# Splitting weight units in halves of two k-tiles, and one sigmoid issued four units later, in a two-block fp32 transformer kernel

## What is computed

```python
def first_block(x, p, ...):
    a = rms_norm(h, norm_mix_pre)
    z = a @ w_in                                   # 2048 x 4656
    y_lru = rglru_mixer(u, g_lru, ...)
    y_nsa = nsa_mixer(q, kc, vc, ksel, vsel, kw, vw, gts, ...)
    h = h + rms_norm(y @ w_out, norm_mix_post)
    f = square(relu(rms_norm(h) @ mlp_w1)) @ mlp_w2    # 2048 x 8192 and back
    h = h + rms_norm(f, norm_mlp_post)
    h = h + sigmoid(h @ ple_gate) * (p @ ple_proj)
def second_block(x, c, ctx, ...):                  # two layers, each on x and on the context ctx
    shift, scale, gate = split(silu(c) @ w_mod + b_mod, 3)
    q, k, v, g_att, u_pool, g_pool, a_conv, b_conv, g_conv = split(hx @ w_in_2, ...)   # 2048 x 6656
    u = a_conv * sigmoid(b_conv); y = depthwise_conv31(u); ...
    y = concat(y_att * silu(g_att), y_pool * silu(g_pool), y_conv * silu(g_conv)) @ w_out_2
```

## Time and profile before

| | |
|---|---|
| median of 3 runs | 2902.8 us |
| the profiled execution's own time | 2906.9 us |
| its span, first to last instruction | 2905.1 us |
| TensorE busy | 2795.1 us, 96% |
| VectorE, ScalarE, GpSimd busy | 1680.8, 1237.5, 316.7 us |
| chain that ended last | TensorE 61%, VectorE 7%, ScalarE 2%, DMA 1% |

### The profile page before, as it was taken

One profiled execution on the slowest core, in us unless ns is written; L12 is line 12 of the kernel. 1 busy time (PEld: TensorE's weight loads), 2 busy tenths in 40 slices (PEclk: granted clock), 3 DMA queues, 4 the chain that ended last, 5 costly groups with the idle time before them and its releaser, 6 DMA issues.

```text
span 2905.1 us, 32293 instructions
## 1 busy us (share of the span) xinstructions
PE 2795.1 (96%) x13403; PEld 2188.4 (75%) x13403; DVE 1680.8 (58%) x1906; ACT 1237.5 (43%) x1493; POOL 316.7 (11%) x260
## 2 busy tenths in 40 slices
PE   4999899999979999999999999999999999999998
PEld 3777788888857777777777787887778788777776
DVE  3545455655545556555444564558885654678754
ACT  3444224544443333333343443444555444444543
POOL 1000100000013000000000020024200011312001
PEclk9999799999989999999999999999999999999999
DMA  6877466446577776676777666565444655553453
GB/s 217 282 252 265 153 210 207 152 145 244 189 245 255 277 243 233 234 248 219 270 250 240 231 212 218 202 231 166 153 134 170 206 185 196 169 168 131 163 172 129
DMA packets 292353, 600.29 MB, mean 207 GB/s; under 512 B 12482, under 2 KB 19210, under 8 KB 290032
## 3 DMA queue, kind: packets, MB, share of 16 engines
q1 hardware_dynamic: 278272, 545.69, 55.6%
q0 software_dynamic: 10960, 49.10, 4.7%
q10 hardware_dynamic: 2976, 3.45, 0.4%
HBM read 585.02 MB, written 13.17 MB: 206 GB/s over the span
## 4 chain that ended last, share of the span: by engine, by line
PE 61%; DVE 7%; ACT 2%; DMA 1%; issue 1%; POOL 0%; ACTq 0%; POOLq 0%; DVEq 0%
PE ps L639 17%; PE ps L641 17%; PE ps L640 17%; DVE wlo L1793 3%; PE ps L650 2%; DVE bvx L2314 2%; ACT whi L1229 1%; PE ps L1043 1%; PE ps L1061 1%; DVE ex L2294 0%; PE ps L1130 0%; PE ps L1154 0%; PE ps L621 0%; PE ps L863 0%; DMA h_d<-h 0%
## 5 line engine op out<-in xcount | busy, mean ns | idle before, releaser
L1793 DVE TENSOR_TENSOR wlo<-raw,whi 128x2048 fp32r<-128x2048 f32 x420 | 973.9, 2319 | 996.2 <-ACT whi L1229 995.4
L1229 ACT ACTIVATE whi<-raw 128x2048 fp32r<-128x2048 f32 x420 | 797.4, 1899 | 1376.6 <-PE ps L641 1165.6
L639 PE MATMUL ps<-whi,ay_hi 128*128 128x512 f32 x1728 | 689.9, 399 | 12.3 <-DVE wlo L1793 8.1
L639 PE MATMUL ps<-whi,ax_hi 128*128 128x512 f32 (+1 forms) x1632 | 652.6, 400 | 25.0 <-DVE wlo L1793 22.7
L641 PE MATMUL ps<-whi,ay_lo 128*128 128x512 f32 x1728 | 675.0, 391 | 0.0
L640 PE MATMUL ps<-wlo,ay_hi 128*128 128x512 f32 x1728 | 674.4, 390 | 0.0
L641 PE MATMUL ps<-whi,ax_lo 128*128 128x512 f32 (+1 forms) x1632 | 637.0, 390 | 0.0
L640 PE MATMUL ps<-wlo,ax_hi 128*128 128x512 f32 (+1 forms) x1632 | 636.1, 390 | 0.0
L639 PEld LDWEIGHTS ps<-whi,ax_hi 128*128 128x128 f32 x1632 | 310.8, 190 | 134.1 <-issue 59.2
L639 PEld LDWEIGHTS ps<-whi,ay_hi 128*128 128x128 f32 x1728 | 325.4, 188 | 94.3 <-issue 14.5
L641 PEld LDWEIGHTS ps<-whi,ay_lo 128*128 128x128 f32 x1728 | 325.1, 188 | 69.4
(11 more groups left out here) (475 smaller groups left out, 1998.1 us busy)
## 6 DMA issues: line engine op xcount, KB each, us to landing
raw<-in_w_in_dram SPq DMA_DIRECT2D x208, 1024.0 KB, 5.1
raw<-in_mlp_w_dram SPq DMA_DIRECT2D x128, 1024.0 KB, 6.4
raw<-in_w_mod_dram SPq DMA_DIRECT2D x96, 1024.0 KB, 7.4
raw<-in_w_out_dram SPq DMA_DIRECT2D x64, 1024.0 KB, 5.1
raw<-in_ple_gate_dram SPq DMA_DIRECT2D x16, 1024.0 KB, 5.1
z2c<-zsc POOLq DMA_DIRECT2D x13, 512.0 KB, 3.3
h<-in_x_dram POOLq DMA_DIRECT2D x2, 2048.0 KB, 10.7
G<-bias_d ACTq DMA_DIRECT2D x4, 768.0 KB, 6.3
```

What stands on the lines that cost most here:

```text
L639: mm(dst, hi_[:, kk, tt], whi[:, x.s % 2, k, 0:w], start=(nth == 0), stop=False)
L1229: A(whi[:, x.s % 2, :, 0:w], raw[:, x.slot, :, 0:w], ACT.Copy).then_inc(hi_ready, 1)
L1793: V.tensor_tensor(wlo[:, x.s % 2, :, 0:w], raw[:, x.slot, :, 0:w], f32v(whi[:, x.s % 2, :, 0:w]), ALU.subtract).then_inc(lo_ready, 1)
```

## The change

Splitting, handing over and freeing go by halves of two k-tiles. ScalarE makes `whi` in two instructions of 1024 elements, each after the same half of unit s-2 has been used; VectorE makes `wlo` in two; TensorE waits for each half apart. `lo_ready`, `hi_ready` and `unit_used` count halves, so every wait on them elsewhere is doubled. TensorE's order inside a unit stays "rows first" in the first and the last unit of a chunk (`by_rows`), and is "half first" in the two between: there the first half of the weights is free in the middle of the unit, and in `by_rows` units after three quarters. ScalarE's sigmoid of `cb` moves from position 0 to position 4 of `context()`, which is from behind the split of MLP2 to behind that of MLP6.

```diff
             def hand_unit(x, A):
-                pe.wait_ge(lo_ready, x.s + 1)
                 hi_, lo_ = A
                 w = x.ph.width
-                for b in range(TB):
+                by_rows = x.u in (0, UPC - 1)
+                for i in range(2 * TB):
+                    b, kh = (i // 2, i % 2) if by_rows else (i % 2, i // 2)
                     a, bank = half(x, b)
-                    if x.u == 0 and a >= 3:
+                    if b == 0:
+                        pe.wait_ge(lo_ready, 2 * x.s + kh + 1)
+                    if x.u == 0 and a >= 3 and kh == 0:
                         pe.wait_ge(half_out, a - 2)
...
-                    for k in range(UK):
+                    for k in range(2 * kh, 2 * kh + 2):
...
-                    if x.u == UPC - 1 and b == 0:
+                    if x.u == UPC - 1 and (b, kh) == (0, 1):
                         ins.then_inc(half_done, 1)
-                ins.then_inc(unit_used, 1)
+                    if b == 1:
+                        ins.then_inc(unit_used, 1)
...
             def hand_split(x):
                 act.wait_ge(raw_in[x.slot], x.landed)
-                if x.s >= 2:
-                    act.wait_ge(unit_used, x.s - 1)
                 w = x.ph.width
-                A(whi[:, x.s % 2, :, 0:w], raw[:, x.slot, :, 0:w], ACT.Copy).then_inc(hi_ready, 1)
+                for kh in range(2):
+                    if x.s >= 2:
+                        act.wait_ge(unit_used, 2 * (x.s - 2) + kh + 1)
+                    A(whi[:, x.s % 2, 2 * kh:2 * kh + 2, 0:w], raw[:, x.slot, 2 * kh:2 * kh + 2, 0:w], ACT.Copy).then_inc(hi_ready, 1)
...
             def context():
-                yield 0
+                yield 4
                 act.wait_ge(ev("e_in"), E_IN["u"])
                 A(cb[:, :, :], cb[:, :, :], ACT.Sigmoid).then_inc(ev("e_sqrt"), 1)
-                for n in range(128):
+                for n in range(5, 128):
...
             def hand_low(x):
-                dve.wait_ge(hi_ready, x.s + 1)
                 w = x.ph.width
-                V.tensor_tensor(wlo[:, x.s % 2, :, 0:w], raw[:, x.slot, :, 0:w], f32v(whi[:, x.s % 2, :, 0:w]),
-                                ALU.subtract).then_inc(lo_ready, 1)
+                for kh in range(2):
+                    ks = slice(2 * kh, 2 * kh + 2)
+                    dve.wait_ge(hi_ready, 2 * x.s + kh + 1)
+                    V.tensor_tensor(wlo[:, x.s % 2, ks, 0:w], raw[:, x.slot, ks, 0:w], f32v(whi[:, x.s % 2, ks, 0:w]),
+                                    ALU.subtract).then_inc(lo_ready, 1)
```

More of the change, by code:

```diff
@@ L568, in _ @@
                     if prev.s is not None:
-                        sp.wait_ge(lo_ready, prev.s + 1)
+                        sp.wait_ge(lo_ready, 2 * prev.s + 2)
                     else:
@@ L1207, in prep @@
                     if pr["units"] and g == 0:
-                        act.wait_ge(unit_used, pr["units"])
+                        act.wait_ge(unit_used, 2 * pr["units"])
                     k = pr["off"] + 2 * g
@@ L1427, in squares @@
                     a, bank = half(chunk(xs, i)[0], b)
-                    act.wait_ge(unit_used, chunk(xs, i)[3].s + 1) if b else act.wait_ge(half_done, a // 2 + 1)
+                    act.wait_ge(unit_used, 2 * chunk(xs, i)[3].s + 2) if b else act.wait_ge(half_done, a // 2 + 1)
                     A(yb[:, b, i * CH:i * CH + CH], ps[:, bank, :], ACT.Square, accum_out=ssq[:, n, b, i:i + 1])\
@@ L1453, in hT_part @@
                 act.wait_ge(hT_psum, c + 1)
-                act.wait_ge(unit_used, MLP[32 * (c // 4)].s)
+                act.wait_ge(unit_used, 2 * MLP[32 * (c // 4)].s)
                 A(ay_hi[:, UK * (c % 4):UK * (c % 4) + UK, :].rearrange("p (a b) c -> p a (b c)", b=2), ps[:, 4:6, :],
@@ L1572, in sigmoids @@
                     a, bank = half(chunk(GATE, i)[0], b)
-                    act.wait_ge(unit_used, chunk(GATE, i)[3].s + 1) if b else act.wait_ge(half_done, a // 2 + 1)
+                    act.wait_ge(unit_used, 2 * chunk(GATE, i)[3].s + 2) if b else act.wait_ge(half_done, a // 2 + 1)
                     if i >= 2:
@@ L1908, in keep @@
                     a = 2 * j + b
-                    dve.wait_ge(unit_used, 4 * j + 4) if b else dve.wait_ge(half_done, j + 1)
+                    dve.wait_ge(unit_used, 8 * j + 8) if b else dve.wait_ge(half_done, j + 1)
                     V.tensor_copy(kept(j)[:, b], ps[:, a % 3, 0:w]).then_inc(half_out, 1)
@@ L2037, in evacuated @@
                 x = chunk(xs, i)
-                dve.wait_ge(unit_used, x[3].s + 1) if b else dve.wait_ge(half_done, x[0].a // 2 + 1)
+                dve.wait_ge(unit_used, 2 * x[3].s + 2) if b else dve.wait_ge(half_done, x[0].a // 2 + 1)
                 return ps[:, half(x[0], b)[1], :]
@@ L2617, in mixing @@
                 end = lambda p: chunk(xs, p)[0].a + 2
-                pool.wait_ge(unit_used, (F1, CTX1)[l][-1].s + 1)
+                pool.wait_ge(unit_used, 2 * (F1, CTX1)[l][-1].s + 2)
                 dma(W.rcn[:, :, :].rearrange("p g t -> p (g t)"), everywhere(I["k_rcount"].rearrange("g t -> (g t)"), 4 * SEQ))\
```

## The result

The changed kernel took 2873.26 us (median of 4 runs, 2869.93 to 2874.99), the kernel before beside it 2903.72 us (2900.07 to 2907.09). The ratio is 0.989, with the interval 0.9879 to 0.9902. That is 30.5 us less; the forecast was 32 us less than the median of the runs shown, 2871 us.

What follows compares the result with a forecast made beforehand. TensorE, busy 96% of the span, was taken as the bound, so only its gaps could be closed. Savings of 12 + 10 + 7 + 2 + 2 - 1 = 32 us from 2902.8 gave 2871 us, range 2858 to 2890.

Steps and rivals of the forecast that it cites:

- Sigmoid, 12 us: Start of the MLP phase: with the sigmoid moved behind MLP6's split, MLP6 begins 12.0 us earlier.
- landed 9.3 us later: MLP3's load, issued at about 818.7, was taken to arrive 9.3 us later, at 828.0.
- no gap: In front of MLP3: its first half ready at 830.4, before TensorE ends MLP2 at 831.0, so no wait.
- rival (b): Sigmoid finds a worse place: MLP6 landing 5 us later makes it worth 7, total 2876 us; chance 0.10.
- two squares of 1.04 us: GpSimd's squares behind the sigmoid's product, done at 857.5; TensorE waits 2.7 us for them before MLP6.
- Other waits for `wlo`, 10 us: TensorE's waits for `wlo` besides MLP3's, mostly in mixing layers: 10 of 14.4 us saved, bounds 5 and 14.
- VectorE steps between units, 7 us: TensorE's waits for VectorE steps between units: steps begin up to 2.0 us earlier, 7 us saved, bounds 2 and 13.
- Boundary, 2 us: Stage boundary after the first product: second half ready 2.0 us earlier, saving 2 us of TensorE's 5.6.
- Clock, 2 us: Lower-clock stretches behind three gaps of about 2 us may go: 2 us saved, bounds 0 and 5.
- Costs, 1 us: VectorE's surcharge for halves in stretches without idle time; TensorE's second wait per unit counted as nothing: 1 us lost.
- rival (c): TensorE's extra wait or bank change costs 0.10 us per unit, 42 us over 420 units: 2913 us; chance 0.05.
- Rival (a): Only the sigmoid's part arrives, VectorE being the bound where TensorE waits: 16 us saved, 2887 us; chance 0.14.

Runs made afterwards that it cites:

- e1: The kernel before with only the sigmoid moved four units later, units whole: 2892.01 us, ratio 0.9967.
- e2: The changed kernel with the sigmoid back at position 0, so only halves: 2876.78 us, ratio 0.9907.
- e3: The changed kernel with the sigmoid at position 2 instead of 4: 2866.54 us, ratio 0.9871.
- e7: The changed kernel, sigmoid at position 4, but GpSimd squares the first chunk before the sigmoid's product: 2866.06 us, ratio 0.9872.
- e9: e8 with GpSimd's product and sum of 1024 columns in the rotary step in four pieces each: 2849.18 us, ratio 0.9812.
- e4: The changed kernel with `by_rows` order (rows first) in every unit: 2873.34 us, ratio 0.9892.
- e5: The changed kernel still splitting in halves, but TensorE waits for the whole unit and frees both halves at its end: 2896.84 us, ratio 0.9981.
- e6: The changed kernel freeing by halves, but TensorE waits for the whole unit before its first matmul: 2885.07 us, ratio 0.9934.
- e10: The changed kernel with units split, handed over and freed in four quarters of one k-tile instead of two halves: 2871.21 us, ratio 0.9884.
- e12: e9 with four quarters in place of two halves: 2853.39 us, ratio 0.9825.
- e8: e3 with GpSimd's sum of the gate rows in eight pieces of 256 columns: 2860.88 us, ratio 0.9854.
- e11: The kernel before, whole units and sigmoid at its old place, with GpSimd's rotary and gate-row work in pieces of 256 columns: 2882.89 us, ratio 0.9926.

## Why the prediction was right, and where it wasn't

The total was 2 us off, and its mechanism was right: units handed over in halves, the sigmoid out of the way of MLP3. That the total is so near is luck in part: of the terms the largest and the third were too big and that of the clock too small, and they made up for each other.

*Sigmoid, 12 us.* Alone it is worth 11.0 us (e1), on top of the halves 3.5. In the two profiles the squares' transposes in front of MLP6 came 18.4 us earlier, of which 10.65 us had been won before the MLP phase: 7.7 us for the forecast's 12, and 5.3 once the half clock behind them is over. Four steps were mis-sized. First, "landed 9.3 us later" was 14.5 us, so the "no gap" in front of MLP3 was 4.69 us, while the forecast gap of 3.9 us at MLP4 did not come. Behind MLP3's gap came a stretch of 3.4 us at half clock, 1.7 us that the forecast didn't have; MLP6's split began 2.1 us later than forecast (840.15 + 10.65 = 850.8 for 848.7). To that extent rival (b) came true, on MLP3's landing and not on MLP6's. I had taken the landing from the kernel before. There SyncE asks for MLP3 0.3 us behind GpSimd's first transfer; in the changed kernel it is 1.0 us behind it. In e1 it is 0.3 us, and there MLP3 landed after 9.6 us again; in e2, e3 and e7 it is 1.0 to 1.1 us, and it landed after 14.4 or 14.5. That GpSimd's transfers then go ahead of MLP3 is what this suggests; no run moved them, so it stays open. Second, the "two squares of 1.04 us" took 2.00 each beside VectorE's splits, 1.9 us more: the new wait was 4.5 us and not 2.7. Third, this wait brought a stretch at half clock, 2.4 us more, and this kind of cost the forecast had only as a bound (3.4 us). Fourth, the same kind behind MLP3, the 1.7 us above. By e3 and e7 the wait for the squares and the half clock behind it are worth 7 us together. MLP3's gap they leave as it is.

*Other waits for `wlo`, 10 us.* They went from 14.4 to 9.5 - 4.7 = 4.8 us: 9.6. Right. Where four waits remained, the forecast had named the place (the mixing phase, VectorE without idle time) but not what fills it; e9 shows that it is GpSimd's long instructions.

*VectorE steps between units, 7 us.* Too big. Of the 21.1 us in the 12 other rows 17.7 are left, the squares not counted: 3.4 us. In VectorE's rows alone it is 16.0 and 12.3 us, 3.7 less, and in e2 the same. The waits on L2280 stayed, because what delays them is a GpSimd instruction that does not begin earlier; those for `ex`, `xq` (L1065) and `modp_a` grew by 5.0 us in all, and the others fell by 8.4. Of the 5.0 us 2.0 are a wait for `modp_a` at 318 us that e2, e3, e4 and e7 don't have. "They begin up to 2.0 us earlier" was true of the split in front of them and not of them.

*Boundary, 2 us.* The one after the first product fell from 5.6 to 4.6 us, in e2 and e7 to 3.7: 0.9 to 1.8 us. The first boundary is 0.4 us longer, as forecast in sign.

*Clock, 2 us.* Undersized. TensorE's busy time fell by 15.9 us between the profiles; about 6 of that is chance (below). The three stretches of 3.4 us at the lower level that followed gaps of about 2 us (near 1466, 2572 and 2801 us) are all gone: 5.1 us, the forecast's upper bound. The two new ones in the MLP phase are what the sigmoid's term lost. Halves alone agree: the median of e2 is 26.3 us below, for 20 forecast. In its profile the waits fell by 18.0 us and TensorE's busy time by 11.4, of which 3.4 are in the stretch near 312 us. The remaining 8 us stand where the forecast had 2.

*Costs, 1 us, and rival (c).* The pitch inside the halved units is 0.227 us as before; TensorE's timeline:

```profile
699.66 0.39 PE L644 MATMUL ps<-whi,ax_lo 128*128 128x512 f32 x1
699.89 0.39 PE L642 MATMUL ps<-whi,ax_hi 128*128 128x512 f32 x1
700.12 0.39 PE L643 MATMUL ps<-wlo,ax_hi 128*128 128x512 f32 x1
```

A second wait per unit that is satisfied costs nothing: over some 2000 matmuls from 400 to 780 us, whole units before and halves after, the changed kernel's lead stays between 10.64 and 10.66 us. But halves without their benefit (e5) did cost some 5 us against e1, where 1 was forecast. That it is the instructions isn't shown: the ranges of the two overlap, and the two waits for `ax_lo` and `ay_lo` of L2287 (L2289 in e5) are 3.4 us each in e5 for 2.1 and 2.2 in e1.

*Rival (a)* had VectorE as the bound where TensorE waits. It was right about the place and wrong about the price. With e6 and the changed kernel 11.8 us apart, the earlier start is worth what (a) denied, but e9 shows that a bound of VectorE was there all the same, and that it was GpSimd's.

## What to carry to other kernels

When a unit of work passes through two engines to a third, hand it over and free it in parts: early freeing and early start were worth 12 us each here, and the dearer instructions showed no cost beside that, as long as the splitting engines have idle time and waits are left to shorten (e10, e12). Before a long VectorE or ScalarE step is moved, follow what is queued behind it on the next engine; here the consumer's consumer, GpSimd's squares, cost 7 of 12 us, and swapping two independent GpSimd jobs got them back. An instruction that takes several times its usual time is worth a look before anything else is tuned: the pieces of e9, found that way, took 17.3 us off e3, and with the sigmoid's better place 24 us off the changed kernel; 2849.18 us is the fastest version here.

## What the runs showed of the hardware

*GpSimd and VectorE hold each other up, here for the length of the other's instruction.* A `TENSOR_TENSOR` of 0.68 us took 5.09 us beside one of GpSimd of 5.55, and 1.23 us when that was cut in eight. Instructions as small as one column are held. VectorE's timeline of the changed kernel:

```profile
2041.19 2.15 DVE L2299 SCALAR_TENSOR_TENSOR stx<-stx,lamc 128x1 f32<-128x1 f32 x1
2043.37 2.92 DVE L2301 SCALAR_TENSOR_TENSOR ex<-ex,stx 128x512 f32<-128x512 f32 x1
```

beside GpSimd's:

```profile
2040.08 3.24 POOL L2662 TENSOR_TENSOR xq<-xq,ropex 128x1024 f32<-128x1024 f32 x1
2043.40 2.34 POOL L2663 TENSOR_TENSOR xq<-xq,rtx 128x1024 f32<-128x1024 f32 x1
```

Both of VectorE's end as GpSimd's end (2043.34 with 2043.32; the second 0.55 us behind 2045.74). In e9 they took 0.22 and 0.75 us; GpSimd had ended its pieces at 2042.11, so these two show the undisturbed length:

```profile
2044.54 0.22 DVE L2299 SCALAR_TENSOR_TENSOR stx<-stx,lamc 128x1 f32<-128x1 f32 x1
2044.79 0.75 DVE L2301 SCALAR_TENSOR_TENSOR ex<-ex,stx 128x512 f32<-128x512 f32 x1
```

The longest of all 32 on each of the two lines was 2.16 and 2.93 us in the changed kernel and is 0.51 and 1.19 in e9. GpSimd is held too. Its instruction at 2040.08 took 3.24 us, where others of its size take as little as 2.34; VectorE's splits were under way when it began and ended at 2041.08, 2.24 us before it did:

```profile
2038.19 2.89 DVE L1800 TENSOR_TENSOR wlo<-raw,whi 128x1024 fp32r<-128x1024 f32 x2
```

The Trainium skill, "SBUF — State Buffer", section "Who interferes with whom", says that a VectorE instruction with two SBUF inputs and a GpSimd instruction that reads SBUF exclude each other for a whole instruction, whichever came first. These rows agree, but for one start: VectorE's second instruction began 0.03 us before GpSimd's by the profile and was still held to its end. Cutting the longer one is the remedy that e8, e9 and e11 measured. It should have stood in my prediction: the earlier trace rows had a tap of 5.89 us in view, and I priced the squares as if nothing ran beside them.

*The clock falls at another moment from run to run.* In the narrow units that begin near 304 us DMA is nearly full, and TensorE's clock falls to the lower level in every profile, but not at the same time, although the changed kernel, e2 and e3 are the same program up to there. The window from 312 to 316 us, in the changed kernel:

```profile
312.00:316.00 4.00, 4.00 (x36) 3.13 (x36) 0.43 (x2) 0.40 (x2) 0.00 (x0) 1.00 1.04 394
```

in e2:

```profile
312.00:316.00 4.00, 4.00 (x21) 2.75 (x20) 0.05 (x1) 0.20 (x1) 0.00 (x0) 0.50 1.05 398
```

and in e3:

```profile
312.00:316.00 4.00, 4.00 (x28) 2.89 (x27) 0.43 (x2) 0.46 (x2) 0.00 (x0) 0.74 0.96 352
```

That is 36, 21 and 28 matmuls in the same 4 us. The clock fell at 316.9 us in the changed kernel, at 309.2 in e2 and 313.9 in e3. In the profile of the kernel before it fell at 305.7, and at the same matmul, the one that the kernel before starts at 320.3, the changed kernel has gained 6.8 us since 304. That needs nothing of the change: e1 and e11 are the kernel before up to there, their clocks fell at 306.9 and 313.5, and they gained 1.1 and 6.6 us. So the two profiles are some 6 us further apart by chance. That is most of the difference between 37.0 us by the spans and 30.5 us by the medians. What sets the moment stays open.
